# Recurrence levels in another step order, feed-forward products with the high and low half of the rows side by side, and ScalarE's tables requested by name

## What is computed

```python
def hgrn2_mixer(cols, lb, o_gain):
    ...
    log_f = jnp.logaddexp(jnp.log(lb), jnp.log1p(-lb) + jax.nn.log_sigmoid(f))
    k = (1.0 - lb) * jax.nn.sigmoid(-f)
    o = gla_chunk_scan(sh(q), sh(k), sh(iv), sh(log_f))   # S_t = diag(f_t) S_{t-1} + k_t^T v_t ; o_t = q_t S_t
    o = rms_norm(o, o_gain)

def gla_mixer(x, w_in, w_gate_up, b_gate, norm_g, w_out):
    q, k, v, r, g_lr = jnp.split(x @ w_in, GLA_SPLITS, axis=-1)
    log_a = jax.nn.log_sigmoid((g_lr @ w_gate_up + b_gate).astype(jnp.float32)) / GLA_TAU
    ...
    decay = jnp.exp(-jnp.abs(L[:, :, :, None, :] - L[:, :, None, :, :]))
    ...

def sq_relu_mlp(x, w1, w2):
    return jnp.square(jax.nn.relu(x @ w1)) @ w2
```

## Time and profile before

| | |
|---|---|
| median of 3 runs | 1936.88 us (1935.88 to 1937.53) |
| the profiled execution's own time | 1935.98 us |
| its span, first to last instruction | 1934.2 us |
| busy: TensorE, its weight loads | 97%, 85% |
| busy: VectorE, ScalarE, GpSimd | 60%, 48%, 31% |
| granted TensorE clock, mean | 0.99 |

### The profile page before, as it was taken

One profiled execution on the slowest core, in us unless ns is written; L12 is line 12 of the kernel. 1 busy time (PEld: TensorE's weight loads), 2 busy tenths in 40 slices (PEclk: granted clock), 3 DMA queues, 4 the chain that ended last, 5 costly groups with the idle time before them and its releaser, 6 DMA issues.

```text
span 1934.2 us, 26975 instructions
## 1 busy us (share of the span) xinstructions
PE 1871.9 (97%) x10912; PEld 1648.9 (85%) x10912; DVE 1169.3 (60%) x1926; ACT 932.3 (48%) x1045; POOL 596.4 (31%) x132
## 2 busy tenths in 40 slices
PE   7999999999898999999999999999999999999998
PEld 6788888879787888999888899889899978889996
DVE  6788778885967688332676422476523277862326
ACT  5555555454453454444454444453444445444443
POOL 0000000000000002878300788500588700058870
PEclk9999999999999999999999999999999999999999
DMA  8343443644232434655453555543655543265551
GB/s 306 131 164 141 174 153 134 224 159 153 109 112 88 154 109 180 215 193 180 154 202 115 196 195 191 200 164 148 238 199 196 189 158 131 90 242 197 196 190 49
DMA packets 53555, 324.93 MB, mean 168 GB/s; under 512 B 8624, under 2 KB 12080, under 8 KB 16208
## 3 DMA queue, kind: packets, MB, share of 16 engines
q1 hardware_dynamic: 45200, 309.97, 44.2%
q10 hardware_dynamic: 8256, 13.58, 2.2%
HBM read 322.48 MB, written 1.05 MB: 167 GB/s over the span
## 4 chain that ended last, share of the span: by engine, by line
PE 86%; DVE 9%; ACT 2%; issue 2%; SPq 1%; DMA 0%; DVEq 0%; ACTq 0%
PE project L997 47%; PE output L997 29%; PE turn L1175 2%; DVE wlo L1716 1%; PE output L1138 1%; PE output L1115 1%; DVE arena L2057 1%; SPq L928 1%; PE output L1234 1%; PE turn L1094 1%; PE output L1123 1%; PE output L1240 1%; DVE arena L2080 1%; DVE arena L2078 1%; DVE arena L1834 0%
## 5 line engine op out<-in xcount | busy, mean ns | idle before, releaser
L965 POOL TENSOR_TENSOR wlo<-raw,whi 128x2048 fp32r<-128x2048 f32 x128 | 596.2, 4689 | 1293.9 <-ACT whi L1356 1276.8
L1356 ACT ACTIVATE whi<-raw 128x2048 fp32r<-128x2048 f32 x291 | 553.3, 1913 | 368.4 <-PE project L997 272.5
L1716 DVE TENSOR_TENSOR wlo<-raw,whi 128x2048 fp32r<-128x2048 f32 x163 | 376.9, 2322 | 47.3 <-ACT whi L1356 43.5
L997 PE MATMUL project<-XTh,whi 128*128 128x256 f32 x1360 | 386.7, 284 | 0.0
L997 PE MATMUL project<-XTl,whi 128*128 128x256 f32 x1360 | 384.8, 283 | 0.0
L997 PE MATMUL project<-XTh,wlo 128*128 128x256 f32 x1360 | 384.8, 283 | 0.0
L2487 DVE TENSOR_TENSOR arena<-arena 128x512 f32<-128x512 f32 x56 | 131.4, 2378 | 399.5 <-ACT arena L1671 399.5
L997 PE MATMUL output<-whi,YTh 128*128 128x512 f32 x736 | 289.7, 394 | 3.7 <-DVE wlo L1716 3.7
L997 PE MATMUL output<-wlo,YTh 128*128 128x512 f32 x736 | 287.7, 391 | 0.0
L997 PE MATMUL output<-whi,YTl 128*128 128x512 f32 x736 | 287.6, 391 | 0.0
L997 PE MATMUL project<-whi,XTh 128*128 128x512 f32 x688 | 280.3, 407 | 4.1 <-ACT arena L1365 3.2
(11 more groups left out here) (258 smaller groups left out, 2093.0 us busy)
## 6 DMA issues: line engine op xcount, KB each, us to landing
raw<-in_units SPq DMA_DIRECT2D x291, 1024.0 KB, 4.8
arena<-in_ln_g ACTq DMA_DIRECT2D x8, 512.0 KB, 5.4
arena<-in_ln_b ACTq DMA_DIRECT2D x8, 512.0 KB, 7.1
tok<-in_mem SPq DMA_DIRECT2D x2, 512.0 KB, 5.8
arena<-in_mem_norm_gain ACTq DMA_DIRECT2D x2, 512.0 KB, 4.8
xres<-in_x SPq DMA_DIRECT2D x1, 1024.0 KB, 12.9
arena<-in_mem ACTq DMA_DIRECT2D x1, 1024.0 KB, 6.4
arena<-in_p ACTq DMA_DIRECT2D x4, 256.0 KB, 3.4
```

Of the source, the lines that this page charges most:

```text
L965: pool.tensor_tensor(wlo[:, slot, :], raw[:, slot, :], whi[:, slot, :], ALU.subtract).then_inc(lo_pool, 1)
L997: mm = pe.matmul(out, x if x_stationary else w, w if x_stationary else x, start=start and i == 0, stop=stop and i == 2, skip_group_check=True)
L1356: act.activation(whi[:, slot, :], raw[:, slot, :], ACT.Copy).then_inc(hi_done, 1)
L1716: dve.tensor_tensor(wlo[:, slot, :], raw[:, slot, :], whi[:, slot, :], ALU.subtract).then_inc(lo_dve, 1)
```

## The change

1. **Feed-forward.** XTh and XTl become the two halves of one tile `XT` (128 x 8 x 2 x 256). In the loop `mlp1` makes for each column block m and row block k one matmul of 512 columns, weights' high with both halves, and one of 256 columns, weights' low with the high half. Each m has a bank of its own, `project` for even and `turn` for odd m: columns 0 to 255 hold high x high, columns 256 to 511 the other two. ScalarE copies the latter into `relu`, VectorE adds the former, and the square becomes max(x, 0) * x in one operation. Chunks 0 and 1 keep the old products.
2. **Order in `levels()`.** A list `lag_to` names for each cover unit the level behind which VectorE makes the low part (before: at once, but for the last two of GLA). A gate's product by VectorE can lag too, while ScalarE's part does not. The last evacuation (`levend`) stands right behind level 8, ahead of the lagging steps. `oscan` waits for the last evacuation in its second half only. Banks of odd and even levels are swapped so that this is possible; in the second hgrn half level 0 uses the banks `turn` and no longer waits for the gate's product.
3. **Around the hgrn levels.** In the first half the low part of one unit goes ahead of the decay gate, and the turn of y's third chunk goes from before the levels to behind level 4. In the second half the low part of the last output units goes ahead of `oscan`. In GLA the weight copy that stood ahead of the keys' copies goes behind them. `glr` and `glagate` swap banks.
4. **Tables.** `preload_act_table_set` asks for the set "natural_log_exp_and_others" ahead of each decay gate, and for "exp_and_others" behind it.

The diff, cut (bank names that only follow from the swap are left out):

```diff
         add(step, n=m, ahead=False if hold[0] else ahead, **f)
-        if hold[0] and lagging[0]:
+        if hold[0] and lag[0] is not None:
             behind.append(lambda: add("ahead", n=m, on="s"))
-            lags.append(lambda: add("ahead", n=m, on="v"))
+            lags.append((lag[0], lambda: add("ahead", n=m, on="v")))
         elif hold[0]:
             behind.append(lambda: add("ahead", n=m, on="sv"))
...
         g, one, scalar_post, _ = pieces(w, col, tag, **f)
         def last():
             one(1)
-            if hold[0]:
+            if hold[0] and lag[0] is not None and tag == "gate":
+                level = lag[0]
+
+                def split_post():
+                    fields = scalar_post(on="s")
+                    lags.append((level, lambda: add("post", on="v", **fields)))
+
+                posts.append(split_post)
+            elif hold[0]:
                 posts.append(scalar_post)
             else:
                 scalar_post()
...
-    def levels(kind, hg, cover, pp=False):
+    def levels(kind, hg, cover, lag_to, pp=False, gq=None, turns=None, ahead_of_scan=None):
 
 
         L = n["L"]
         every = 9 / (len(cover) + 1)
         at = [int((i + 1) * every) - (kind == "hgrn") for i in range(len(cover))]
-        gq = n["pd"]
+        gates = n["pd"]
         for l in range(9):
             hold[0] = True
             while at and at[0] <= l:
-                lagging[0] = kind == "gla" and len(at) <= 2
                 at.pop(0)
+                lag[0] = lag_to.pop(0)
                 cover.pop(0)()
+                lag[0] = None
             hold[0] = False
-            if l == 8 and lags:
-                lags.pop(0)()
-            add("lev", kind=kind, hg=hg, l=l, L=L + l, heads=len(heads), gq=gq, pp=pp)
+            add("lev", kind=kind, hg=hg, l=l, L=L + l, heads=len(heads), gq=gates if gq is None else gq, gates=gates, pp=pp, t=n["t"])
+            if l == 8:
+                add("levend", kind=kind, hg=hg, L=L + 8, pp=pp)
             release()
+            if turns is not None and l == 4:
+                turns()
+            for x in [x for x in lags if x[0] <= l]:
+                lags.remove(x)
+                x[1]()
         n["L"] += 9
-        while lags:
-            lags.pop(0)()
-        while cover:
-            cover.pop(0)()
         release()
-        add("levend", kind=kind, hg=hg, L=L + 8, pp=pp)
+        for x in lags:
+            x[1]()
+        lags.clear()
+        if ahead_of_scan is not None:
+            ahead_of_scan()
         add("oscan", kind=kind, hg=hg, L=L + 9, vg=n["vtok"], j=n["gla"], pp=pp)
...
+    project(wb, 0, "fq", feature_major=True, scale=1.0, hg=0, second=0, behind_post="s",
+            between=lambda: (drain(), add("ymul", chunk=2, layer=1, second=0), add("ahead", n=len(units), on="v"),
                              add("fgate", hg=0, part=0, gf=gf, heads=len(heads))))
     add("fgate", hg=0, part=1)
     add("z0", gq=n["pd"])
     n["vtok"], c1 = cover_of(wb, 2048 + 512, "vtok", c=1)
-    for h in range(H2):
-        turn("y", h, 2, "Y", 8)
     c1[0]()
-    levels("hgrn", 0, c1[1:] + cover_of(wb, 3584, "gate", buf="y", gh=0)[1])
+    levels("hgrn", 0, c1[1:] + cover_of(wb, 3584, "gate", buf="y", gh=0)[1], [3, 8, 8],
+           turns=lambda: [turn("y", h, 2, "Y", 8) for h in range(H2)])
     gf = project(wb, 1024 + 512, "f", feature_major=True, hg=1)
...
+    gq = n["pd"]
     _, one, scalar_post, _ = pieces(wb, 3584 + 512, "gate", buf="y", gh=1)
     one(0)
     one(1, ahead="s")
     behind.append(lambda m=len(units) - 1: add("ahead", n=m, on="v"))
     scalar_post()
     g, one, tail = begin_output(("w_out_b", 0), 1536)
-    levels("hgrn", 1, [lambda: one(0, first=True), lambda: one(1), lambda: one(4)], pp=True)
+    levels("hgrn", 1, [lambda: one(0, first=True), lambda: one(1), lambda: one(4)], [3, 5, 8], pp=True, gq=gq,
+           turns=None, ahead_of_scan=lambda: add("ahead", n=len(units), on="v"))
     one(5, ahead="s")
     for h in range(H2):
         turn("y", h, 1, "Y", 4)
-    add("ahead", n=len(units) - 1, on="v")
...
-        one(1)
+        one(1, ahead="v")
         add("post", g=0, tag="glagate", j=j, part=1, src_n=0, on="v", scaled=None)
         scalar_post()
+        add("ahead", n=len(units) - 1, on="s")
         cv = cover_of(w, 1024, "vtok", c=0)[1]
         n["vtok"], more = cover_of(w, 1024 + 512, "vtok", c=1)
         cv += more
         cg = cover_of(w, 2048, "gate", buf="G", gh=0)[1]
-        levels("gla", 0, cv + cg)
+        levels("gla", 0, cv + cg, [None, None, None, None, 7, 8])
...
-        XTh, XTl = sb("XTh", [P, 8, S], F32R), sb("XTl", [P, 8, S], F32R)
+        XT = sb("XT", [P, 8, 2, S], F32R)
+        XTh, XTl = XT[:, :, 0, :], XT[:, :, 1, :]
...
+        def level_bank(f, l):
+
+            return PP[l % 2] if f["pp"] else PQ[2 * (1 - l % 2)]
+
+        def level_banks(f, l):
+
+            if f["pp"]:
+                return PT if l == 0 else PP
+            return PQ[2 * (1 - l % 2):2 * (1 - l % 2) + 2]
+
+        def scan_bank(f, h):
+
+            return PP[1 - h] if f["pp"] else PQ[h]
...
-                    if f["pp"] and l < 2:
+                    if f["pp"] and l == 0:
                         pe.wait_ge(lev_evac, L)
+                        for t in range(2):
+                            wait_bank(f["t"] + t)
+                    elif f["pp"] and l == 1:
+                        for b in range(2):
+                            pe.wait_ge(p_evac[b], f["gates"])
                     elif L >= 2:
                         pe.wait_ge(lev_evac, L - 1)
-                    banks = PP if f["pp"] else PQ[2 * (L % 2):2 * (L % 2) + 2]
+                    banks = level_banks(f, l)
...
-                    pe.wait_ge(lev_evac, f["L"])
                     for b in range(2):
                         pe.wait_ge(p_evac[b], f["vg"] + 1)
                     AT = (ATG if g else ATB).rearrange("p (j x t) -> p j x t", j=4, x=3)
                     w = 256 if g else 128
                     for h in range(H2):
+                        pe.wait_ge(lev_evac, f["L"] - 1 + h)
                         for j in range(4):
                             col = j * w + (0 if g else f["hg"] * 512)
-                            bank = 2 * h + j // 2 if g else h
-                            o = (PP if f["pp"] else PQ)[bank][:, (j * w) % 512:(j * w) % 512 + w]
+                            bank = PQ[2 * h + j // 2] if g else scan_bank(f, h)
+                            o = bank[:, (j * w) % 512:(j * w) % 512 + w]
...
                     def mlp1(n, slot, g):
                         for u in range(2):
-                            project_unit(n + u, (slot + u) % RING, g, u, True, pool_less=less)
+                            pe.wait_ge(lo_pool, n + u - less)
+                            begin[0] = True
+                            wh = whi[:, (slot + u) % RING, :].rearrange("p (k c) -> p k c", k=4)
+                            wl = wlo[:, (slot + u) % RING, :].rearrange("p (k c) -> p k c", k=4)
+                            for m in range(4):
+                                b = m // 2
+                                if u == 0 and m % 2 == 0:
+                                    pe.wait_ge(p_evac[b], g)
+                                bank = (PP, PT)[m % 2][b]
+                                ms = slice(m * P, (m + 1) * P)
+                                for k in range(4):
+                                    mm = pe.matmul(bank[:, :], wh[:, k, ms], XT[:, 4 * u + k].rearrange("p a s -> p (a s)"),
+                                                   start=u == 0 and k == 0, stop=False, skip_group_check=True)
+                                    if begin[0]:
+                                        mm.then_inc(unit_begun, 1)
+                                        begin[0] = False
+                                for k in range(4):
+                                    mm = pe.matmul(bank[:, S:2 * S], wl[:, k, ms], XTh[:, 4 * u + k, :], start=False,
+                                                   stop=u == 1 and k == 3, skip_group_check=True)
+                                if u == 1 and m % 2 == 1:
+                                    mm.then_inc(p_done[b], 1)
...
                 if tag == "glagate":
+                    act.preload_act_table_set("natural_log_exp_and_others")
                     act.wait_ge(v2a, nth("v2a"))
                     act.activation(DG, DG, ACT.Exp, scale=-1.0).then_inc(act_own, 1)
                     last.own()
                     act.wait_ge(*last.at)
                     act.activation(DG, DG, ACT.Ln, bias=1.0).then_inc(a2v, 1)
                     last.other(a2v, nth("a2v"))
+                    act.preload_act_table_set("exp_and_others")
...
                 elif kind == "fgate":
+                    act.preload_act_table_set("natural_log_exp_and_others")
...
+                    act.preload_act_table_set("exp_and_others")
                 elif kind == "lev":
...
```

(16 more changed lines are left out.)

45 lines of the change are left out of this document (19 added, 26 removed).

## The result

The changed kernel takes **1911.56 us** (median of 4 runs, 1911.05 to 1912.67) where the kernel before takes 1937.2 beside it: ratio 0.9866, 95% interval 0.9851 to 0.9881. Forecast were 1903.8 us and a range of 1892 to 1914. So 25.6 us came where 33.1 were forecast. Two executions of the experiments further down, of 3765 and 6328 us, were disturbed and stand in no median, ratio or clock here. The profiled executions differ by 23.3 us of span (1934.2 to 1910.9), and that sum can be laid out by stages.

A forecast was written before the change was run, and what follows sets the result against it. TensorE is busy nearly everywhere, so only less TensorE work or fewer waits help; feed-forward 10.3, first half 10.7, second half with output 7.1 and GLA 5.0 sum to 33.1 us, from 1936.88 to 1903.8 us, range 1892 to 1914.

The forecast's parts named there:

- Feed-forward, 10.3 forecast: Feed-forward loop, four layers: wide and narrow products save 0.43 us a chunk, 10.3 us in all, 7.7 as lower bound.
- a pair (k, m) gets one of each, 0.346: Feed-forward loop: one 512-column and one 256-column matmul take 0.346 us in place of three 256-column ones at 0.360.
- GpSimd runs ahead: some 5.8 us: Feed-forward: GpSimd's low part is done some 5.8 us before it is wanted, which hides 0.6 us over six chunks.
- First half, 10.7 forecast: First hgrn half with its scan: fewer waits and half of 2.85 us of clock gain 10.7 us, bounds 9.2 and 12.1.
- two signs of being wrong: GpSimd's feed-forward idle growing beyond 5 us, or the clock falling in the levels without a long wait ahead of it.
- Second half, 3.8 forecast: Second hgrn half: reordered levels gain 3.8 us, half of 2.95 us of clock kept as lost, bounds 2.3 and 5.3.
- The output behind it, 3.3 forecast: Output behind the second scan: the 3.7 us low-part wait goes, 1.8 stay; 3.3 us gained with clock, 1.9 to 4.7.
- GLA, 5.0 forecast: Both GLA layers: 1.3 us from VectorE's earlier chain and 1.2 at the scan in each, 5.0 us in all.
- (1): Feed-forward rival: adds are held by GpSimd as the squares are, 2.6 us a layer lost, 1924 us; chance 0.10.
- (4): Feed-forward rival: adds and squares lengthen GpSimd's ring, which decides from 24.3 us on; 1948.5 us, slower; chance 0.04.
- (2): Clock rival: it stays low around and behind both scans and falls again in GLA; 25.4 us gained, 1911.5; chance 0.17.
- (3): Recurrence rival: the order does nothing, VectorE's total work sets the levels; only feed-forward's 10.3 us stay, 1926.6; chance 0.06.

The follow-up runs named there:

- Grouping: Changed kernel with all 16 wide products ahead of the 16 narrow ones in each unit of the loop's first product; 1910.39 us, ratio 0.9860.
- adds from SBUF: Changed kernel with ScalarE also copying the high x high halves out of PSUM, so VectorE's adds have both operands in SBUF; 1950.07 us, ratio 1.0060.

## Why the prediction was right, and where it was off

The gain came where it was forecast, and three quarters of it. By the profiles 9.8 us are missing of 33.1: 3.6 in the feed-forward, 0.8 in the first half, 3.9 in the second, 1.3 in GLA and 1.5 of clock ahead of the recurrence, while the output gave 1.4 more.

**Feed-forward, 10.3 forecast, 6.7 measured: two steps.** The term "a pair (k, m) gets one of each, 0.346" was mis-sized. The passage from narrow to wide costs 0.02 us, not nothing, and not the 0.013 of the bound (which gave 7.7 and was itself too high). Grouping showed that it is the passages. The second step is "GpSimd runs ahead: some 5.8 us". That lead is there in the loop (5.5 us), but not for the last pair, which waits for the low parts of both its units at once and so wants the last one 5.4 us sooner than the loop would. Its margin is 0.2 us (1.4 before the change), as the wait of 0.49 shows as soon as the chunk is 0.12 shorter, and the 6.3 where the ring is 1.1 longer and the loop itself waits 0.26. Grouping gained 6 x 0.12 - 0.49 = 0.23 us a layer, so with a chunk of 21.95, too, the term would have stood near 6.7 + 4 x 0.23 = 7.6 (an estimate). That the last pair asks for one unit at a time would take the wait away, but no run tried it. That the adds run free and the squares don't was right to the row (0.42 us, 3.70 idle).

The Trainium skill (GPSIMD Engine Reference, Specifications, the row on SBUF interfaces) names two SBUF inputs as what contends with GpSimd. By that rule, the runs agree: 0.41 us with one operand in PSUM, 4.83 with both in SBUF.

**First half, 10.7 forecast, 9.9 measured.** Waits fell from 62.10 - 53.46 = 8.6 us to 1.6 (2.2 forecast to stay), and the first spell of low clock went with its wait. The spell around the scan stayed whole (clock 0.66 from 520 to 530, 3.4 us lost), of which the forecast had kept half. This is one of the two signs of being wrong that the prediction named, a fall in the levels without a long wait ahead of it, and it came: the wait is 0.7 us. The time is right in spite of it, since the spell costs 3.4 us only.

**Second half, 3.8 forecast, nothing measured.** This is where the sum failed. Waits fell from 5.5 us to 4.3, not to 2.5: 2.20 us for the copies and 2.15 at levels 2, 7 and 8, where VectorE was assumed less late. The clock, instead of giving back half, fell behind three waits (0.91 in place of 0.94). **The output behind it, 3.3 forecast, 4.7 measured:** the low part's wait went as said (1.46 us is left, 1.8 forecast), and the clock came back whole.

**GLA, 5.0 forecast, 1.1 and 2.6 measured.** Here the forecast's reasoning held. VectorE's chain, from the gate's first operation to level 4, took 35.3 us (665.80 to 701.06) and takes 34.0 (652.77 to 686.75), 1.3 less in both layers, as forecast; the copies' wait fell from 2.72 to 1.07, and 2.35 came at level 4.

```profile
652.77 1.74 DVE L1941 TENSOR_SCALAR arena<-output,arena 128x256 f32<-128x256 f32 x4 [4.19 <-PE output L1307]
```

From level 4 to GpSimd's first unit it was 57.7 us in both layers. In the second layer it is 56.3, 1.4 less (1.2 forecast); in the first it is 58.0, since the clock falls behind the wait. The prediction had that case at 0.8 a layer. Before, the clock was low in both layers too, but ahead of level 4, where TensorE waited for VectorE all the same. In the second profile of the changed kernel the clock fell in both layers.

**Rivals.** (1) and (4), adds held and a ring too long, did not come, but adds from SBUF show that both were one operand away, and that the ring decides from about 22.1 us, by the last pair, not from 24.3. (2), the clock, came in half: around the first scan and in one GLA layer, but not behind the second scan. Its 1911.5 hits the median, by another sum: it had the full 10.3 in it. (3) is refuted: order and requests together gave 11 us at full clock.

The Trainium skill (ScalarE: Activation LUTs, What ACT_TABLE_LOAD costs) adds 1.38 us of drain to a load. No run shows one: the load starts at 549.99, 0.02 us behind the copy that ends at 549.97, and Exp starts at its end, 551.28; and with the requests left out VectorE's way from the GLA gate to level 4 is longer by 1.3 us, the load alone (653.75 to 688.99).

## What to carry over

- A ring of one engine's work that depends on another's is to be checked behind its loop, too: look at what the last steps wait for and what margin the last unit has. Here the loop had 5.5 us and the pair behind it 0.2, since it waits for two units at once.
- Where a profile has stretches of low clock, compare span times mean clock besides medians. It shows savings of 2 us that executions 5 us apart hide. It isn't the time, though: the requests for tables save 1.8 us in it and none that shows in the ratio.
- A short wait in the midst of the levels costs its length and up to 3.4 us more of clock. Move one low part (3.4 us at full clock) or fill the wait with idle products, and check what is late next.

## What the runs showed of the hardware

- An operation of VectorE with both operands in SBUF took 4.83 us instead of 0.41 beside GpSimd's instructions of 4.6 us each, and 0.41 again once GpSimd had stopped.
- The combined table set served Exp, Ln and the copies behind them; leaving out the reload moved a load to the next gate's product.
- The same program has its stretches of low clock at partly different places in each execution; executions of one kernel spread by up to 10 us for it while full-clock time spread by 4.4 at most. Behind a wait of 2.3 to 2.7 us the clock fell in 9 of 14 places, behind one of 0.3 to 0.7 us at the same place in none of 10. Three products of 512 columns put into waits of 0.7 and 0.3 us kept the clock at 2.4 GHz around the first scan, where it had fallen in all eleven other profiles with the new order (in one of them half as long).
